# Eight level products and the values' transposes of an HGRN2 head moved later in TensorE's hand-written order of a head's second pair

## The chip, the cores and the metric

The kernel runs on one core of a Trainium2 chip. The metric is the device time of one execution in microseconds (us). TensorE multiplies (PE in the rows, PEld for its weight loads), VectorE is DVE, ScalarE is ACT, GpSimd is POOL, SyncE (SP) issues most DMAs.

## The reference

Two decoder layers over 512 prompt tokens and 8 x 4 sample tokens (544 columns), width 2048: an RWKV-7 layer and then an HGRN2 layer, each with a projection in, a recurrence, a gate and a projection out. The HGRN2 layer has 16 heads of 128 keys by 128 values. What matters here, cut down:

```python
q, f_logit, i, z = jnp.split(x @ w_in, 4, axis=-1)
f = lb + (1.0 - lb) * jax.nn.sigmoid(f_logit)
log_f = jnp.log(jnp.maximum(f, GATE_FLOOR))
k = (1.0 - lb) * jax.nn.sigmoid(-f_logit)
q = jax.nn.silu(q) * HGRN_DK ** -0.5
# per chunk and head, G = cumsum(log_f):
dec = jnp.where(mask, jnp.exp(jnp.minimum(G_t - G_s, 0.0)), 0.0)
A = jnp.einsum('bhtd,bhsd,bhtsd->bhts', q_c, k_c, dec)
o = A @ v_c + (q_c * exp(G)) @ S
S = exp(G_last) * S + (k_c * exp(G_last - G)).T @ v_c
...
o = o * lax.rsqrt(jnp.mean(o * o, axis=-1, keepdims=True) + NORM_EPS) * norm_w
out = (o * jax.nn.silu(z)) @ w_o
```

## The kernel before, in words

Everything stands channels by tokens: a tile of 128 output channels by 544 tokens, computed as two halves of 272 tokens in two banks. Matrix products are made of three passes with operands split in a high part (made by ScalarE, `_hi`) and a low part (made by VectorE as the difference, `_lo`): high x high, high x low, low x high.

HGRN2 needs four such tiles for each head: forget gate F, query qr, value v, gate zs. For heads e = 1 to 14 (14 heads) they are computed two at a time: pair 2e - 2 makes F and qr, pair 2e - 1 makes v and zs. `seven_products(q, steps)` is one pair. It computes a 2 x 2 block product (two output tiles, two halves of the tokens) over 12 of the 16 input tiles with seven products instead of eight, by sums of weight tiles and sums of token halves, and the other four input tiles (`rest`) in the plain way. Its order is written out by hand, in 58 sub-steps of three products of 128x272 each:

- product 0: sub-steps 1 to 6; product 1: 7 to 12; rest(0, 0): 13 to 16; rest(0, 1): 17 to 20
- product 2: 21 to 26; product 3: 27 to 32; product 4: 33 to 38; product 5: 39 to 44
- rest(1, 1): 45 to 48; product 6: 49 to 54; rest(1, 0): 55 to 58

The dictionary `steps` names a sub-step after which another piece of the head's work is put into TensorE's queue. TensorE works its queue in order, so a piece that has to wait holds up all that follows. The pieces are:

- `level(e, n)` for n = 0 to 7 (L1753, products at L1777, L1780, L1785, L1790): the products of keys and queries inside blocks that double from level to level. Level 0 needs the SiLU of qr; level 1 needs Q = qr x F; level n from 2 needs the keys and queries as `widen(e, n - 2)` left them (L2478, products at L2496, L2498, L2500 of VectorE), and the bank of level n - 2 taken over by `take(e, n - 2)` (L2502).
- `v_by_token`, `k_by_token` (L1794, L1806): transposes of values and keys; `kv` (L1815): products of the two. ScalarE copies the transposes out (`v_copy`, `k_copy`).
- `late(e - 1)` of the head before: two `outputs`, four `sample_out`, `sample_state`, and `norm`, which sums the squares of the head's output.

In the first pair of head e stand the keys' transposes and `kv` of head e - 1 and then its eight late pieces; in the second pair stand the eight levels of head e and the transposes of its values.

ScalarE and VectorE have their own orders written out, in `gates_pair(e, q)` and `values_pair(e, q)`. Both hold, between the head's own operations, what the products need: `item_hi`/`item_lo` (high and low part of one of seven weight items of 128x768, L1957 and L2300; item k is needed from product k on), `rest_hi`/`rest_lo` (128x512, L1965 and L2304), `weight_sum_1` to `_4` (VectorE), and the moves of finished sums out of the banks: `first_out` (L1969), `second_out` (L1973), `third_out` (L1977) on ScalarE, `upper_first` (L2338), `upper_fifth` (L2343), `upper_second` (L2348, L2351), `lower_second` (L2356, L2358), `lower_first` (L2362) on VectorE. Product 2 may start when `first_out` is done, as it adds onto the bank that this one copies:

```python
pe.wait_ge(s.p1, q + 1)
product(2, X, False)
```

On ScalarE, in `values_pair`, the order up to there is: item 2, SiLU of qr, `first_out`. In `gates_pair` the late part is `second_out`, item 5, `head_root` (Ln L2113 and Exp L2116 of what `norm` summed), item 6, rest, `third_out`, item 0 of the next pair, the two sigmoids, item 1 of the next pair; VectorE's `finish` stands after item 6 and ahead of `upper_second`. Before a function of another kind ScalarE loads a table (ACT_TABLE_LOAD in the rows).

SyncE loads a pair's two weight tiles (`next_weights`): the first once items 2 to 4 of the pair before are made, the second once item 6 is split. Heads 0 and 15 go through plain dense tiles, and the change doesn't touch them, but the last pair makes the high and low part of the dense tile behind it (`split_hi(GE)`, `split_lo(GE)`, 128x2048).

Of the kernel before, what the change touches and what calls it, by code (L numbers as in the profile page):

```python
# [1392 lines left out]
def trunk(nc, keep, d):  # L1393

    with ExitStack() as ctx:
# [10 lines left out]
        F, K, Q, qr, v, zs, sq, rs = (sb(n, [P, T]) for n in ("F", "K", "Q", "qr", "v", "zs", "sq", "rs"))  # L1406
# [47 lines left out]
        NQ = (GE - GS) // 2  # L1454
# [145 lines left out]
        def _(pe):  # L1600
# [48 lines left out]
            def seven_products(q, steps):  # L1649
                X, Y, V = (banks[(q + i) % 3] for i in range(3))  # L1650
                Z = banks[3]
                at = itertools.count(1)

                def three_passes(out, hi, lo, n, x, start):
                    w = slice(n * P, n * P + P)
                    for m, (a, b) in enumerate(((hi[:, w], x[0]), (hi[:, w], x[1]), (lo[:, w], x[0]))):
                        mm = pe.matmul(out, a, b, start=start and m == 0, stop=(m == 2), skip_group_check=True)  # L1657
                    return mm

                def then_step():  # L1660
                    m = next(at)
                    if m in steps:
                        steps[m]()

                def product(k, out, start):
                    pe.wait_ge(s.it_hi, ITEMS * q + k + 1)
                    pe.wait_ge(s.it_lo, ITEMS * q + k + 1)
                    hi, lo = item_slot(q, k)
                    for j in range(U):
                        mm = three_passes(out, hi, lo, j, operand(k, j), start and j == 0)  # L1670
                        if j == U - 1:
                            mm.then_inc(s.used, 1)
                        then_step()

                def rest(i, a, out, start, sem):
                    for n, kt in enumerate(range(2 * U, KT)):
                        mm = three_passes(out, c_hi[i], c_lo[i], n, base(kt, a), start and n == 0)
                        if sem and kt == KT - 1:
                            mm.then_inc(sem, 1)
                        then_step()  # L1680

                if q == 0:
                    pe.wait_ge(s.evac, GS - 1)
                    pe.wait_ge(s.t_lo, 2 * U)
                else:
                    pe.wait_ge(s.f0, q)
                product(0, X, True)
                if q:
                    pe.wait_ge(s.g1, q)
                product(1, Y, True)  # L1690
                pe.wait_ge(s.c_hi, 2 * q + 1)
                pe.wait_ge(s.c_lo, 2 * q + 1)
                rest(0, 0, Y, False, None)
                if q == 0:
                    pe.wait_ge(s.evac, GS)
                else:
                    pe.wait_ge(s.c12, q)
                rest(0, 1, Z, True, s.c_used)
                pe.wait_ge(s.p1, q + 1)
                product(2, X, False)  # L1700
                if q:
                    pe.wait_ge(s.evac, GS + 2 * q)
                product(3, V, True)
                pe.wait_ge(s.u2, q + 1)
                if q == 0:
                    pe.wait_ge(s.t3_lo, U)
                product(4, X, False)
                product(5, Z, False)
                pe.wait_ge(s.c_hi, 2 * q + 2)
                pe.wait_ge(s.c_lo, 2 * q + 2)  # L1710
                pe.wait_ge(s.up, q + 1)
                rest(1, 1, V, False, s.v_ready)
                pe.wait_ge(s.u3, q + 1)
                product(6, X, False)
                rest(1, 0, X, False, s.c_used)
# [78 lines left out]
            def v_by_token(e):  # L1794
                pe.wait_ge(s.evac, H0 + 4 * e + 3)
                if e:
                    pe.wait_ge(s.oln, 2 * e)
                else:
                    pe.wait_ge(s.rstd, 2)
                for c in range(4):  # L1800
                    pe.transpose(blk(tok_ps, c), blk(v, c), k.ident[:, :])  # L1801
                for h in range(2):
                    mm = pe.matmul(sm_ps[SMP * h:SMP * h + SMP, 0:P], v[:, SEQ:T], k.ident[:, :], start=True, stop=True)
                mm.then_inc(s.vt_mm, 1)
# [56 lines left out]
            def late(e):  # L1861
                return [lambda: outputs(e, 0), lambda: outputs(e, 2), lambda: sample_out(e, 0),
                        lambda: sample_out(e, 1), lambda: sample_out(e, 2), lambda: sample_out(e, 3),
                        lambda: sample_state(e), lambda: norm(e)]
# [8 lines left out]
            for e in range(KT):  # L1873
                n = H0 + 4 * e
                L = lambda m: (lambda: level(e, m))
                keys = [lambda: k_by_token(e - 1), lambda: kv(e - 1)]
                if 1 <= e < KT - 1:
                    steps = dict(zip((10, 13, 15, 17, 19, 21, 24, 27), late(e - 1)))
                    if e > 1:
                        steps.update(zip((2, 6), keys))  # L1880
                    seven_products(2 * e - 2, steps)
                    steps = {m: L(i) for i, m in enumerate((10, 12, 18, 24, 30, 36, 42, 48))}
                    seven_products(2 * e - 1, {**steps, 53: lambda: v_by_token(e)})
                    continue
                if e:
                    dense_evens_last(n, dict(zip((0, 2, 5, 6, 7, 8, 9, 10, 12, 15), keys + late(e - 1))))
                    dense(n + 1, {})
                at = (4, 5, 8, 11, 14) if e else (6, 7, 9, 12, 14)
                dense(n + 2, {kt: L(m) for m, kt in enumerate(at)})
                dense(n + 3, {1: L(5), 3: lambda: v_by_token(e), 6: L(6), 9: L(7), 12: lambda: k_by_token(e),  # L1890
                              15: lambda: kv(e)})
# [43 lines left out]
        def _(act):  # L1935
# [214 lines left out]
            def values_pair(e, q):  # L2150
                item_hi(q, 2)
                act.wait_ge(s.evac, H0 + 4 * e + 2)
                act.wait_ge(s.q1s, q)
                silu(qr, s.qr)
                act.wait_ge(s.vt_mm, e)
                first_out(q, v)
                item_hi(q, 3)
                item_hi(q, 4)
                rest_hi(q, 1)
                second_out(q, v)  # L2160
                item_hi(q, 5)
                item_hi(q, 6)
                if q < NQ - 1:
                    rest_hi(q + 1, 0)
                act.wait_ge(s.yz, e)
                third_out(q, zs)
                if q < NQ - 1:
                    item_hi(q + 1, 0)
                else:
                    split_hi(GE)  # L2170
                blocks_out(e)
                level_out(e, 6)
                if q < NQ - 1:
                    item_hi(q + 1, 1)
                level_out(e, 7)
                v_copy(e)

# [73 lines left out]
            for a in range(2):  # L2251
                for n in range(2):
                    m = KT - 2 + n
# [34 lines left out]
        def _(dve):  # L2288
# [283 lines left out]
            def values_pair(e, q):  # L2572
                lower_first(q - 1, qr)
                weight_sum_3(q)
                item_lo(q, 2)
                weight_sum_4(q)
                first_q(e)
                item_lo(q, 3)
                take(e, 0)
                widen(e, 0)  # L2580
                rest_lo(q, 1)
                item_lo(q, 4)
                take(e, 1)
                widen(e, 1)
                upper_first(q, v)
                take(e, 2)
                widen(e, 2)
                item_lo(q, 5)
                take(e, 3)
                widen(e, 3)  # L2590
                upper_fifth(q, v)
                item_lo(q, 6)
                take(e, 4)
                widen(e, 4)
                if q < NQ - 1:
                    rest_lo(q + 1, 0)
                    item_lo(q + 1, 0)
                else:
                    split_lo(GE)
                take(e, 5)  # L2600
                widen(e, 5)
                upper_second(q, v)
                if q < NQ - 1:
                    item_lo(q + 1, 1)
                widen(e, 6)
                lower_second(q, zs)
                if q < NQ - 1:
                    weight_sum_1(q + 1)
                    weight_sum_2(q + 1)
# [233 lines left out]
```

## Time and profile before

| | |
|---|---|
| Median of 3 runs | 2952.1 us (2946.95 to 2952.74) |
| Profiled execution | 2950.76 us, its span 2948.9 us |
| Mean granted TensorE clock | 0.969 of full speed |
| TensorE busy, products | 2759.2 us, 94% of the span |
| VectorE busy | 1592.5 us, 54% |
| ScalarE busy | 1260.1 us, 43% |
| GpSimd busy | 118.6 us, 4% |
| HBM | 91 GB/s over the span |

The profile is that of one execution. Busy time of TensorE is counted from the start of a product to its modelled end; products overlap, so a busy TensorE need not run at its full rate, and the clock must be read beside it. Times in the rows count from the span's start.

### The profile page before, as it was taken

The page shows a single profiled execution, that of the slowest core. Times are in us where ns is not written, and L with a number is a line of the kernel's source. Part 1 is how long each engine was busy: PE and PEld are TensorE (multiplying, and loading weights), DVE is VectorE, ACT ScalarE, POOL GpSimd, SP SyncE. Part 2 cuts the span into 40 slices and gives each one's busy share as a digit, 9 for nine tenths or more (in the row PEclk, how much of TensorE's full clock was granted, in tenths as well). Part 3 has the DMA queues.
Part 4 walks back from the last instruction along what each step waited for, and adds up shares of the span by engine and source line. Part 5 has one row for each costly group of instructions (what it writes and reads, how often), then busy time and mean ns, then how long its engine had stood idle before and what let it go on. Part 6 is the DMA issues. An engine that isn't in the chain of part 4 may idle for free. (4 is left out here: it accounts for less than half of the span.)

```text
span 2948.9 us, 82517 instructions
## 1 busy us (share of the span) xinstructions
PE 2759.2 (94%) x36816; PEld 2595.7 (88%) x36816; DVE 1592.5 (54%) x2703; ACT 1260.1 (43%) x1869; POOL 118.6 (4%) x92
## 2 busy tenths in 40 slices
PE   6999999999999999999799879989999998999997
PEld 5899999999997888887799778888888888888997
DVE  6334323333227788887522566666666666664324
ACT  5344424234225555555322454444444444444322
POOL 0000000000000000000000000000000000000000
PEclk8999999999999999999999989999999999999999
DMA  3333333333311111112222322322222222224323
GB/s 122 125 97 111 111 109 109 111 113 137 107 53 52 52 52 52 52 56 68 87 92 94 128 74 77 108 89 82 92 77 92 77 95 92 92 84 171 118 88 111
DMA packets 86816, 273.48 MB, mean 93 GB/s; under 512 B 16448, under 2 KB 29504, under 8 KB 65984
## 3 DMA queue, kind: packets, MB, share of 16 engines
q1 hardware_dynamic: 77248, 250.37, 25.5%
q10 hardware_dynamic: 9216, 17.83, 1.6%
q8 instruction: 292, 4.78, 0.7%
q14 instruction: 60, 0.49, 0.1%
HBM read 221.63 MB, written 46.54 MB: 91 GB/s over the span
## 5 line engine op out<-in xcount | busy, mean ns | idle before, releaser
L136 PE MATMUL w_pair<-a_x_hi,keep_w_hi 128*128 128x272 f32 x2016 | 427.4, 293 | 20.3 <-DVE a_x_lo L1059 19.4
L136 PE MATMUL w_pair<-a_x_lo,keep_w_hi 128*128 128x272 f32 x2016 | 418.7, 289 | 0.0
L136 PE MATMUL w_pair<-a_x_hi,keep_w_lo 128*128 128x272 f32 x2016 | 416.4, 288 | 0.0
L1045 DVE TENSOR_TENSOR keep_w_lo<-keep_raw,keep_w_hi 128x2048 fp32r<-128x2048 f32 x63 | 144.4, 2292 | 469.8 <-ACT keep_w_hi L798 469.8
L136 PEld LDWEIGHTS w_pair<-a_x_hi,keep_w_hi 128*128 128x128 f32 x2016 | 319.3, 189 | 26.7 <-issue 21.7
L136 PEld LDWEIGHTS w_pair<-a_x_lo,keep_w_hi 128*128 128x128 f32 x2016 | 317.1, 189 | 0.0
L136 PEld LDWEIGHTS w_pair<-a_x_hi,keep_w_lo 128*128 128x128 f32 x2016 | 316.9, 188 | 0.0
L136 PE MATMUL t_pair<-t_x_hi,keep_w_hi 128*128 128x272 f32 x1216 | 262.7, 298 | 27.1 <-DVE t_x_lo L2411 9.1
L136 PE MATMUL t_pair<-t_x_lo,keep_w_hi 128*128 128x272 f32 x1216 | 253.8, 290 | 0.0
L136 PE MATMUL t_pair<-t_x_hi,keep_w_lo 128*128 128x272 f32 x1216 | 253.6, 290 | 0.0
L136 PEld LDWEIGHTS t_pair<-t_x_hi,keep_w_hi 128*128 128x128 f32 x1216 | 193.0, 191 | 35.9 <-issue 19.9
L812 ACT ACTIVATE a_stage<-w_pair 128x544 f32<-128x544 f32 x64 | 40.0, 625 | 425.0 <-PE w_pair L136 425.0
L1657 PE MATMUL t_pair<-t_x_hi,u_it_hi 128*128 128x272 f32 x672 | 206.6, 307 | 0.0
L1657 PE MATMUL t_pair<-t_x_hi,u_it_lo 128*128 128x272 f32 x672 | 197.5, 294 | 0.0
L1657 PE MATMUL t_pair<-t_x_lo,u_it_hi 128*128 128x272 f32 x672 | 197.5, 294 | 0.0
L136 PEld LDWEIGHTS t_pair<-t_x_lo,keep_w_hi 128*128 128x128 f32 x1216 | 194.7, 191 | 0.0
L136 PEld LDWEIGHTS t_pair<-t_x_hi,keep_w_lo 128*128 128x128 f32 x1216 | 192.8, 190 | 0.0
L1657 PE MATMUL t_pair<-u_To,u_it_hi 128*128 128x272 f32 x896 | 183.6, 299 | 0.0
L1657 PEld LDWEIGHTS t_pair<-u_To,u_it_hi 128*128 128x128 f32 x896 | 140.7, 188 | 15.6 <-issue 13.4
L1657 PE MATMUL t_pair<-t_x_hi,u_c_hi 128*128 128x272 f32 x448 | 145.6, 325 | 0.0
L1657 PE MATMUL t_pair<-t_x_lo,u_c_hi 128*128 128x272 f32 x448 | 136.3, 304 | 0.0
L1657 PE MATMUL t_pair<-t_x_hi,u_c_lo 128*128 128x272 f32 x448 | 135.3, 302 | 0.0
(448 smaller groups left out, 6092.3 us busy)
## 6 DMA issues: line engine op xcount, KB each, us to landing
keep_raw<-in_w_in SPq DMA_DIRECT2D x64, 1024.0 KB, 5.0
keep_raw<-in_hgrn_in SPq DMA_DIRECT2D x64, 1024.0 KB, 5.1
keep_raw<-in_rwkv_wo SPq DMA_DIRECT2D x16, 1024.0 KB, 5.0
keep_raw<-in_hgrn_wo SPq DMA_DIRECT2D x16, 1024.0 KB, 5.0
t_Ss<-in_hgrn_s SPq DMA_DIRECT2D x16, 512.0 KB, 7.2
out_hgrn_s<-t_Sd SPq DMA_DIRECT2D x16, 512.0 KB, 7.7
scr_r<-a_stage ACTq DMA_DIRECT2D x16, 272.0 KB, 2.2
scr_k<-a_stage ACTq DMA_DIRECT2D x16, 272.0 KB, 2.1
```

The costliest lines, as they stand in the source:

```text
L136: mm = pe.matmul(out[:, a, 0:TH], w, x[:, kt, a * TH:(a + 1) * TH], start=(kt == order[0] and n == 0), stop=(kt == order[-1] and n == 2))
L812: act.activation(halves(stage[n % 2][:, :]), pair[3 if n == 2 else n % 2][:, :, 0:TH], func).then_inc(p.evac, 1)
L1045: dve.tensor_tensor(w_lo[b][:, :], raw[n % 2][:, :], w_hi[b][:, :].bitcast(F32), ALU.subtract).then_inc(p.raw_lo, 1)
L1657: mm = pe.matmul(out, a, b, start=start and m == 0, stop=(m == 2), skip_group_check=True)
```

## The change

In the second pair of a head the levels go from sub-steps 10, 12, 18, 24, 30, 36, 42, 48 to 22, 25, 31, 36, 41, 46, 51, 55, and the values' transposes from 53 to 58, the pair's last sub-step. In the first pair the keys' transposes and `kv` of the head before go from sub-steps 2 and 6 to 3 and 8, and its eight late pieces from 10, 13, 15, 17, 19, 21, 24, 27 to 13, 16, 18, 20, 22, 24, 27, 30. ScalarE makes the high part of the next pair's item 1 ahead of the copies of the finished blocks instead of between levels 6 and 7. VectorE's order in `values_pair` is written anew: `take` and `widen` of each level stand later among the low parts, and `lower_second` and item 1 of the next pair stand ahead of `take` 5. No operation is added or removed, and the order in which products are summed in a bank stays.

```diff
@@ TensorE @@
-                    steps = dict(zip((10, 13, 15, 17, 19, 21, 24, 27), late(e - 1)))
+                    steps = dict(zip((13, 16, 18, 20, 22, 24, 27, 30), late(e - 1)))
                     if e > 1:
-                        steps.update(zip((2, 6), keys))
+                        steps.update(zip((3, 8), keys))
                     seven_products(2 * e - 2, steps)
-                    steps = {m: L(i) for i, m in enumerate((10, 12, 18, 24, 30, 36, 42, 48))}
-                    seven_products(2 * e - 1, {**steps, 53: lambda: v_by_token(e)})
+                    steps = {m: L(i) for i, m in enumerate((22, 25, 31, 36, 41, 46, 51, 55))}
+                    seven_products(2 * e - 1, {**steps, 58: lambda: v_by_token(e)})
@@ ScalarE, values_pair @@
                 if q < NQ - 1:
                     item_hi(q + 1, 0)
+                    item_hi(q + 1, 1)
                 else:
                     split_hi(GE)
                 blocks_out(e)
                 level_out(e, 6)
-                if q < NQ - 1:
-                    item_hi(q + 1, 1)
                 level_out(e, 7)
@@ VectorE, values_pair @@
                 item_lo(q, 3)
+                rest_lo(q, 1)
+                item_lo(q, 4)
+                upper_first(q, v)
                 take(e, 0)
                 widen(e, 0)
-                rest_lo(q, 1)
-                item_lo(q, 4)
                 take(e, 1)
                 widen(e, 1)
-                upper_first(q, v)
+                item_lo(q, 5)
+                upper_fifth(q, v)
                 take(e, 2)
                 widen(e, 2)
-                item_lo(q, 5)
+                item_lo(q, 6)
                 take(e, 3)
                 widen(e, 3)
-                upper_fifth(q, v)
-                item_lo(q, 6)
-                take(e, 4)
-                widen(e, 4)
                 if q < NQ - 1:
                     rest_lo(q + 1, 0)
                     item_lo(q + 1, 0)
                 else:
                     split_lo(GE)
+                upper_second(q, v)
+                take(e, 4)
+                widen(e, 4)
+                lower_second(q, zs)
+                if q < NQ - 1:
+                    item_lo(q + 1, 1)
                 take(e, 5)
                 widen(e, 5)
-                upper_second(q, v)
-                if q < NQ - 1:
-                    item_lo(q + 1, 1)
                 widen(e, 6)
-                lower_second(q, zs)
```

## Rows read from the trace of the kernel before

**Rows 1.** The page, part 1: busy time, share, instructions of each engine.
```profile
PE 2759.2 (94%) x36816; PEld 2595.7 (88%) x36816; DVE 1592.5 (54%) x2703; ACT 1260.1 (43%) x1869; POOL 118.6 (4%) x92
```

**Rows 2.** TensorE's waits, 1750 to 2660: us in total, times, longest.
```profile
PE t_lev L1777 <- issue: 55.5, 14, 4.0
PE t_lev L1828 <- DVE t_S L2524: 2.5, 13, 0.2
PE t_lev L1790 <- DVE t_Q L2498: 1.2, 1, 1.2
```

**Rows 3.** The chain that ended last, whole span: start, us, what.
```profile
1773.39 15.49 PE t_pair L1657 x123
...
2615.97 15.49 PE t_pair L1657 x123
```

**Rows 4.** The same chain, from 2140 to 2210, one inner head.
```profile
2162.07 15.41 PE t_pair L1657 x123
2177.48 4.01 issue
2181.49 0.66 PE t_lev L1777 x26
...
2182.20 1.66 PE t_pair L1657 x6
...
2184.53 3.65 PE t_pair L1657 x18
...
2191.08 0.39 PE t_lev L1777 x32
2191.46 2.46 PE t_pair L1657 x18
...
2205.93 2.84 PE t_pair L1657 x21
```

**Rows 5.** Windows: stretch, length, busy time by engine, PEclk, DMA share, GB/s.
```profile
2177.50:2181.40 3.90, 0.00 (x0) 0.00 (x0) 3.71 (x6) 2.78 (x4) 0.00 (x0) 0.86 0.00 0
2181.50:2187.00 5.50, 5.50 (x85) 5.12 (x86) 4.51 (x10) 2.25 (x4) 0.00 (x0) 0.50 0.62 191
2187.20:2203.00 15.80, 15.80 (x253) 14.63 (x252) 10.67 (x30) 5.87 (x13) 1.90 (x1) 1.00 0.20 68
...
2654.90:2657.60 2.70, 1.50 (x12) 1.28 (x11) 2.70 (x6) 0.64 (x3) 0.00 (x0) 1.00 0.93 310
```

**Rows 6.** ScalarE's timeline, 2140 to 2210: start, us, line and operation.
```profile
2161.57 1.28 ACT L2113 ACT_TABLE_LOAD   x1
2162.86 0.87 ACT L2113 ACTIVATE t_rs<-t_tok,keep_eps 128x272 f32<-128x272 f32 x2
...
2180.73 0.66 ACT L2066 ACTIVATE t_qr<-t_qr 128x544 f32<-128x544 f32 x1
2181.29 0.37 ACT L1969 COPY t_v<-t_pair 128x272 f32<-128x272 f32 x1
...
2206.46 0.26 ACT L2091 COPY t_vtok<-t_tok 64x128 f32<-64x128 f32 x1
```

**Rows 7.** VectorE's timeline, 2140 to 2210, the same columns.
```profile
2198.06 0.68 DVE L2304 TENSOR_TENSOR u_c_lo<-keep_raw,u_c_hi 128x512 fp32r<-128x512 f32 x1
...
2199.37 0.96 DVE L2300 TENSOR_TENSOR u_it_lo<-keep_raw,u_it_hi 128x768 fp32r<-128x768 f32 x1 [0.62 <-ACT u_it_hi L1957]
2200.24 0.30 DVE L2509 COPY_PREDICATED t_Dg<-t_k_h_lev,t_lev 128x128 f32<-128x128 int32 x1
2200.44 0.42 DVE L2496 TENSOR_TENSOR t_K<-t_K,t_E 128x256 f32<-128x256 f32 x1
...
2201.19 0.43 DVE L2348 TENSOR_TENSOR t_v<-t_pair,t_v 128x272 f32<-128x272 f32 x1
2201.73 0.73 DVE L2351 TENSOR_TENSOR t_v<-t_v,t_rstd 128x544 f32<-128x544 f32 x1
```

**Rows 8.** DMA issues, 2170 to 2240: count, KB each, median us to landing.
```profile
keep_raw<-in_hgrn_in SPq DMA_DIRECT2D x4, 1024.0 KB, 5.3
```

## The prediction

> **What bounds the kernel now.** I read the page first: TensorE is busy for 2759.2 of 2948.9 us [rows 1], so only what stops or slows TensorE counts. Then the list of TensorE's waits over the stretch of the paired heads: one row carries it, 55.5 us in 14 waits of 4.0 us, all ahead of the first product of `level` (L1777) [rows 2]. The whole chain then gives the rhythm: the run that ends in this wait starts at 1773.39 for the first paired head and at 2615.97 for the fourteenth, so a head lasts (2615.97 - 1773.39) / 13 = 64.81 us [rows 3]. I take one inner head apart, around 2180 us, in the chain of that stretch [rows 4]. TensorE runs 41 sub-steps without a break (123 products in 15.41 us, 0.376 us a sub-step of three), stops at 2177.48 for 4.01 us, and then runs slowly: 6 products take 1.66 us and 18 take 3.65 us, where 18 take 2.46 us later on.
>
> The reason for the second loss is in the windows [rows 5]: the granted clock is 0.86 on average while TensorE stands still, 0.50 from 2181.5 to 2187.0 (the 1.2 GHz level) and 1.00 (2.4 GHz) after that. Against the full-rate rows (18 products and a restart 2.46, a middle level 0.39) the slow stretch costs 3.65 - 2.46 = 1.19 for the 18, 1.66 - 0.95 = 0.71 for the 6 (0.95 is 0.75 and a restart of 0.20), and by the same comparison about 0.5 for the two levels in it: 2.4 us. The stop itself costs 4.07 us: the 4.01 of the row, and the little by which two products otherwise overlap.
>
> What ends the stop: the timeline of ScalarE [rows 6]. Level 0 needs the SiLU of the queries, which starts at 2180.73 and ends at 2181.39; level 0 starts at 2181.49 [rows 4]. Followed back, the SiLU stands behind its table load, that behind the copy of item 2, which waits for VectorE's weight sum, and so on: sums, gate, sigmoids, `finish`, the head's Exp and Ln. That chain is a chain of ScalarE and VectorE and hangs on `norm` of the head before (sub-step 27 of the first pair), not on where level 0 stands.
>
> **The change, part by part.** I put all times in the clock of this head. The second pair starts (P1) 10 sub-steps ahead of 2177.48, at 2173.72.
>
> 1. Level 0 from sub-step 10 to 22. At full rate sub-step 20 ends at 2177.48 + 10 x 0.3765 = 2181.25. The stop at 10 is gone. Next late: product 2 begins at sub-step 21 and adds onto a bank that `first_out` has to copy out first, and `first_out` stands behind the SiLU on ScalarE: it started at 2181.29 and ended at 2181.66 [rows 6]. That is already after 2181.25.
>
> 2. `norm` from sub-step 27 to 30. From its end to P1 there are now 28 sub-steps instead of 31, so relative to P1 it ends at 2173.72 - 28 x 0.3765 = 2163.18 instead of 2162.07. Ln started at 2162.86, when its table load (2161.57, 1.28 us) was over and not when `norm` was [rows 4, 6]. Now `norm` is last: Ln at about 2163.25, and everything after it, down to the SiLU and `first_out`, comes 0.4 us later. I find no slack in that chain; where an engine waits, it waits for the other one. So `first_out` ends at 2182.06 and product 2 starts at 2182.16; it would have started at 2181.09, as a product starts about 0.16 us before the end of the one before it. New stop: 1.07 us. Bounds: 0.67 if the 0.4 us is absorbed; 2.35 if a whole table load (1.28) comes onto the chain. I take the chain as it adds up.
>
> The Trainium skill (ScalarE: Activation LUTs, What ACT_TABLE_LOAD costs) puts a switch at 2.66 us, 1.28 of load and 1.38 of drain. The rows show the function starting 1.29 us after its load [rows 6], so I take that; by the page (an estimate) the new stop would be 1.38 us longer in each head and the time 2896 us.
>
> 3. The levels at 25, 31, 36, 41, 46, 51, 55. TensorE needs 0.59 us more for a middle level (0.39 and a restart) [rows 4], and 0.64 for levels 0 to 2, which have a product for the sample tokens as well. Going on from product 2 at 2182.16: level 0 after sub-step 22 at 2183.05; sub-step 25 ends at 2184.82, 31 at 2187.72, 36 at 2190.24, 41 at 2192.71, 46 at 2195.18, 51 at 2197.65, 55 at 2199.75. VectorE has less room, as the levels now stand 5 sub-steps apart (2.47 us) and its other work lies between them. From level 4 on I add its queue in the new order, by start-to-start times of its rows (a row's duration less an overlap of 0.09) [rows 7]: `widen` 3 from 2193.17 (0.75), `rest_lo` 0.60 and `item_lo` 0.87 to 2195.39, `upper_second` 0.54 + 0.63 to 2196.56, `take` 4 0.20, `widen` 4 0.75 (its query product is done at 2197.52, in time for level 6), `lower_second` 0.83 (two half products like the first of `upper_second`), `item_lo` 0.87 to 2199.21, `take` 5 0.20, query product of `widen` 5 done at 2200.17. Level 7 needs that and starts at 2200.25 instead of 2199.70: a wait of 0.5 us. Earlier levels find their operands ready, by 0.8 us (level 2) or more. ScalarE's item copies and VectorE's low parts are ready for products 3 to 6 by a microsecond or more. Bounds of this term: 0 and, with another microsecond in VectorE's queue, 1.5 us.
>
> 4. `v_by_token` from 53 to 58, `k_by_token` from 2 to 3, `kv` from 6 to 8, outputs from 10 to 13. The products are the same, so TensorE's work stays. `v_copy` ends 0.8 us after the transposes (2206.72 against 2205.93) [rows 6]; three sub-steps and a restart give 1.33 us, so `k_by_token` finds it done, with 0.5 us to spare. The weight sums run 1 us later against the pair's start, but item 2 of the next pair is used 21 sub-steps on. S for the first outputs comes, by the same adding, about 5.9 us after the pair's start (before 5.7) and the outputs at sub-step 13 want it at 6.8 (before 5.5), so TensorE's small wait there goes (0.19 us idle, 2.5 us in 13 waits [rows 2]; with the restart 0.35 us of the pace).
>
> 5. DMA: nothing is added. The second weight tile of a pair may be loaded once item 6 has been split; that is now about 9 us ahead of the sum that reads it, and a load lands in about 5.3 us [rows 8]. SyncE's other waits (`sd`, `so_mm`, `yz`) move by at most 1.2 us.
>
> 6. The last paired head: `split_lo(GE)` (2048 columns) stood ahead of `take` 5 and held level 7 up for 1.2 us [rows 2]; now it stands ahead of `upper_second` and by the same adding holds level 6 up by about 0.8 us. With the hand-over to the next dense tile I give that head 1.3 us more gain than the others; the first head has no wait for S and gains 0.35 less.
>
> Sum for an inner head: removed 4.07 + 2.4 + 0.35 = 6.82, which would leave 64.81 - 6.82 = 58.0; added 1.07 + 0.5 = 1.57; net 5.25 us, a head of 59.6. Over 14 heads 73.5 us, plus 1.3 and less 0.35: 74.5 us. The profiled execution took 2950.8 us (span 2948.9 and 1.9 around it), 1.3 below the median 2952.1. So 2876.3 for such an execution, 2877.6 for the median; I forecast 2877.
>
> **The clock.** That the 2.4 us go rests on the stop of 1.07 us leaving the clock up. In this trace an idle of 1.25 us inside the window from 2654.90 kept a granted clock of 1.00 [rows 2, 5], while the 4 us stop lost it. The new stop is nearer to the former.
>
> **Rivals.**
> A: the clock still falls in each head, on the shorter stop together with the small level products behind it. It gives back 14 x 2.4 = 34 us: 2911. For it: the stop recurs every head and the levels follow at once. Against it: levels every 2.8 us run at 1.00 in the trace [rows 5]. The Trainium skill (TensorE: Matmul & The Clock Gate, What's actually happening and HAM oscillation) says the gate judges recent activity on a clock of its own, so by it some heads could fall and others not, between 2877 and 2911. Chance 0.12 for most heads falling.
> B: VectorE's queue is tighter than I add it: the levels wait 1 to 3 us in all per head, or the SiLU chain slips by a table load. 14 x 1.3 to 14 x 3 us back: 2895 to 2919. For it: I count 14 us of VectorE work in about 14.4 us. Chance 0.10.
> C, slower: the compressed stair. `take` and `widen` stand behind low parts that wait for ScalarE's copies, which wait for products 2 and 3, which now come after levels; if every level from 2 to 7 waits 1.3 us more (7.8 us a head), the head is 58.0 + 1.07 + 7.8 = 66.9 us and the time 2952 + 14 x 2 = 2981. It decides from 5.75 us of level waits a head; I add 0.5. Chance 0.03.
> D, no effect: the SiLU itself moves back with level 0, because it hangs on something that TensorE releases late in the pair. Then the 4 us only change their place: 2952. Against it: everything on ScalarE ahead of the SiLU is released before sub-step 10. Chance 0.02.
>
> **How the numbers follow.** Forecast 0.73, its own range 2856 (no stop at product 2 and no wait of level 7: 14 x 1.57 = 22 us less, 2855) to 2895. With A and most of B the range is 2856 to 2912. 0.2% of this kernel is 6 us, about what a measurement tells from no change. Faster 0.95 (forecast, A, B), same 0.02 (D), slower 0.03 (C).
>
> **What would show it.** The wait row of L1777 gone from 4.0 us; in its place an idle of about 1 us ahead of product 2, behind ScalarE's copy of `first_out` (L1969); a granted clock of 1.00 through the head; a head of 59 to 60 us; a wait of L1790 of a few tenths on VectorE's L2498; Ln starting at the end of `norm`. A granted clock near 0.95 over a head, or waits ahead of several levels, would make it wrong.

## The result and the profile after

The changed kernel takes 2883.64 us in the median of 4 runs (2882.63 to 2887.73), the kernel before 2952.42 us in 4 runs: a ratio of 0.9772, 95% interval 0.9755 to 0.9789, so 68.8 us or 2.3% faster. The forecast was 2877 with a range of 2856 to 2912. The profiled execution took 2883.76 us, its span 2882.0.

The page of the changed kernel, parts 1 and 2, against [rows 1]:

```profile
PE 2731.2 (95%) x36816; PEld 2568.2 (89%) x36816; DVE 1608.4 (56%) x2703; ACT 1259.1 (44%) x1869; POOL 117.8 (4%) x92
...
PEclk8999999999999999999999989999999999999998
```

TensorE's waits in the stretch of the paired heads, 1750 to 2600, changed kernel (in total, times, longest), against [rows 2]:

```profile
PE t_pair L1657 <- ACT t_v L1969: 11.2, 14, 0.9
PE t_lev L1790 <- DVE t_Q L2497: 6.4, 13, 0.5
PE t_lev L1785 <- DVE t_K L2495: 4.9, 12, 0.4
PE t_lev L1785 <- DVE t_Q L2497: 1.1, 1, 1.1
PE t_lev L1785 <- issue: 0.3, 1, 0.3
```

The row of 55.5 us is gone, and so is that of the paired heads' outputs (L1828). Three small waits stand in their place: product 2 for `first_out`, level 7 and level 6 for VectorE's widenings (VectorE's line numbers are one lower in the changed kernel). The rows of L1785 with 1.1 and 0.3 us are those of single heads; 1.1 is the last paired one.

The length of a head is best read from ScalarE's copy of the transposed values, which comes once in each. Timeline of ScalarE, changed kernel (start, us), heads 1, 6 and 7:

```profile
1815.91 0.59 ACT L2090 COPY t_vtok<-t_tok 128x512 f32<-128x512 f32 x1 [1.32 <-PE t_tok L1803]
...
2116.21 0.59 ACT L2090 COPY t_vtok<-t_tok 128x512 f32<-128x512 f32 x1 [1.33 <-PE t_tok L1803]
...
2176.25 0.59 ACT L2090 COPY t_vtok<-t_tok 128x512 f32<-128x512 f32 x1 [1.33 <-PE t_tok L1803]
```

The copy of head 13 starts at 2536.59: (2536.59 - 1815.91) / 12 = 60.06 us a head, where the same copy gives 64.83 in the kernel before. So an inner head gains 4.77 us. From the copy of head 0 to that of head 15 the gain is 68.0 us: 14 times 4.77, and 1.2 more. The part ahead of head 0's copy took 1.0 us longer in this execution (1748.8 us against 1747.8), which leaves the 66.9 by which the spans differ. All further heads are read in this way; a difference of 0.1 us a head shows there, while the copy of head 0 comes anywhere from 1743.6 to 1752.4 us in the traces here.

The granted clock, in windows of the changed kernel (columns as in [rows 5]):

```profile
2146.00:2153.00 7.00, 7.00 (x58) 7.00 (x58) 6.18 (x11) 1.98 (x3) 0.00 (x0) 1.00 0.49 173
2153.00:2154.80 1.80, 1.03 (x9) 0.81 (x7) 1.70 (x3) 1.79 (x4) 0.00 (x0) 1.00 0.00 0
2155.00:2156.00 1.00, 1.00 (x35) 0.85 (x38) 0.91 (x2) 1.00 (x2) 0.00 (x0) 1.00 0.36 57
```

The second window holds the stop ahead of product 2. The clock is at its upper level before, in and behind it, and 1.00 over the window from 1760 to 2560.

Where the levels wait: VectorE's timeline in the changed kernel,

```profile
2161.87 0.95 DVE L2299 TENSOR_TENSOR u_it_lo<-u_wS,u_it_hi 128x768 fp32r<-128x768 f32 x1
...
2163.45 1.41 DVE L2495 TENSOR_TENSOR t_K<-t_K,t_E 128x256 f32<-128x256 f32 x1
2164.78 0.41 DVE L2497 TENSOR_TENSOR t_Q<-t_Q,t_E 128x256 f32<-128x256 f32 x1
```

and GpSimd's at the same time:

```profile
2162.03 2.55 POOL L2277 TENSOR_TENSOR t_Sd<-t_Ss,t_E 128x1024 f32<-128x1024 f32 x1 [43.98 <-DVE t_E L2499]
```

The key product of `widen` 2, 0.42 us elsewhere [rows 7], takes 1.41 us. It starts while GpSimd's product for the sample states runs, and ends 0.28 us after that one does (2162.03 + 2.55 = 2164.58). In the kernel before, the same GpSimd product (2189.75, 1.90 us) fell mostly into time that VectorE spent waiting for a level.

### The profile page after: what moved, and what is told of

It is laid out like the page before. It is cut to its first block and busy times, and to the rows that moved or that the text cites. A ratio compares the mean times of both kernels' runs of the same rounds, so it can differ in the third digit from the quotient of the medians.

```text
span 2882.0 us, 82517 instructions
## 1 busy us (share of the span) xinstructions
PE 2731.2 (95%) x36816; PEld 2568.2 (89%) x36816; DVE 1608.4 (56%) x2703; ACT 1259.1 (44%) x1869; POOL 117.8 (4%) x92
## 5 line engine op out<-in xcount | busy, mean ns | idle before, releaser
L1045 DVE TENSOR_TENSOR keep_w_lo<-keep_raw,keep_w_hi 128x2048 fp32r<-128x2048 f32 x63 | 144.4, 2293 | 470.1 <-ACT keep_w_hi L798 470.1
L1657 PE MATMUL t_pair<-t_x_hi,u_it_hi 128*128 128x272 f32 x672 | 200.5, 298 | 0.0
L1657 PE MATMUL t_pair<-t_x_hi,u_c_hi 128*128 128x272 f32 x448 | 135.6, 303 | 0.0
L798 ACT CAST keep_w_hi<-keep_raw 128x2048 fp32r<-128x2048 f32 x63 | 120.2, 1908 | 31.0 <-ACT a_stage L812 28.0
L2293 DVE TENSOR_TENSOR keep_w_lo<-keep_raw,keep_w_hi 128x2048 fp32r<-128x2048 f32 x38 | 87.1, 2292 | 82.2 <-ACT keep_w_hi L1945 82.2
```

What stands on the lines that cost most here:

```text
L798: act.copy(w_hi[2 if n == 2 else n % 2][:, :], raw[n % 2][:, :]).then_inc(p.raw_hi, 1)
L1045: dve.tensor_tensor(w_lo[b][:, :], raw[n % 2][:, :], w_hi[b][:, :].bitcast(F32), ALU.subtract).then_inc(p.raw_lo, 1)
L2293: dve.tensor_tensor(w_lo[g % 2][:, :], raw[g % 2][:, :], w_hi[g % 2][:, :].bitcast(F32), ALU.subtract).then_inc(s.raw_lo, 1)
```

## The experiments

**Is the long row GpSimd's doing?** `sd_later`:

```diff
+ pool.wait_ge(s.o_mm, e + 1)        # heads 1 to 14, and behind Vm
  pool.tensor_tensor(Sd[:, :, :], Ss[:, :, :], E[2]...)
```

GpSimd makes its product for the sample states later here: behind its product `Vm` of the sample tokens' values, and once the head's outputs are done.

> The changed kernel with one edit: for heads 1 to 14 GpSimd's product for the sample states (t_Sd, 128x1024) waits for the head's outputs in the next pair instead of starting behind the second widening. Theory 1: the key product of the third widening takes 1.41 us instead of 0.42 because GpSimd's product runs at the same time, and this 1.0 us in VectorE's queue makes the wait of level 6 (0.41 us). Then that row falls back to 0.42, level 6 no longer waits, level 7 still waits about 0.5 us, a head takes 59.5 instead of 60.04 us and the time is 7 us less, about 2877. Rival: the long row has another cause, or the queue has other room; then a head stays at 60.0 and the time at 2884.

2874.97 us, ratio 0.9747 (0.9733 to 0.9762); a head of 59.65 us. TensorE's waits, 1750 to 2660:

```profile
PE t_pair L1657 <- ACT t_v L1969: 11.8, 14, 0.9
PE t_lev L1790 <- DVE t_Q L2507: 6.4, 13, 0.5
PE t_lev L1828 <- DVE t_S L2533: 1.1, 1, 1.1
PE t_lev L1785 <- DVE t_Q L2507: 0.8, 1, 0.8
```

and the key products of `widen` 2 and `widen` 3 in VectorE's timeline:

```profile
2156.70 0.42 DVE L2505 TENSOR_TENSOR t_K<-t_K,t_E 128x256 f32<-128x256 f32 x1
...
2159.18 0.43 DVE L2505 TENSOR_TENSOR t_K<-t_K,t_E 128x256 f32<-128x256 f32 x1 [0.50 <-PE t_lev L1777]
```

The product is back at 0.42 us and level 6 waits in the last paired head alone. Level 7 waits as before. GpSimd's product cost 0.41 us of a head, the wait of level 6, as theory 1 has it. Most of the other 0.6 us of its 1.0 lay in slack: without it `widen` 3 waits 0.50 us for level 4, and with it `widen` 3 doesn't wait.

**Does the wait of product 2 cost what it shows?** `first_out_first`, and `both_moves` with both edits:

```diff
                 item_hi(q, 2)
+                act.wait_ge(s.vt_mm, e)
+                first_out(q, v)
                 act.wait_ge(s.evac, H0 + 4 * e + 2)
                 act.wait_ge(s.q1s, q)
                 silu(qr, s.qr)
-                act.wait_ge(s.vt_mm, e)
-                first_out(q, v)
```

> The changed kernel with one edit: in the second pair ScalarE copies the first sum out (first_out) ahead of the queries' SiLU instead of behind it. Theory 1 (the waits add up): the wait of product 2, 0.8 us a head, goes, and up to 0.3 us comes back at level 0; 14 x 0.6 = 8 us less, about 2875. Theory 2 (VectorE's queue sets the end of the pair): TensorE comes earlier to levels 6 and 7 and waits there for what it gained at product 2; the time stays within 3 us of 2884, and the waits of L1785 and L1790 grow from 0.4 and 0.5 us to 1.7 us together.

> The changed kernel with both edits: GpSimd's sample-state product behind the next pair's outputs, and first_out ahead of the SiLU. If the two costs are separate they add: a head of 58.9 us, about 2868. If VectorE's queue sets the end of the pair, it is the better of the two alone and no more: 2875 to 2877.

`first_out_first`: 2873.65 us, ratio 0.9742 (0.9726 to 0.9758), a head of 59.41. `both_moves`: 2871.03 us, ratio 0.9733 (0.9719 to 0.9748), a head of 59.00. TensorE's waits of `both_moves`:

```profile
PE t_lev L1790 <- DVE t_Q L2507: 6.5, 13, 0.5
PE t_lev L1777 <- issue: 3.3, 14, 0.2
```

0.65 us for the one edit, 0.41 for the other, 1.06 for the two: they add. (The whole times, 10.0, 8.7 and 12.6 us under the changed kernel's, scatter too much to show it.) The waits of levels 6 and 7 did not take up the gain (6.8 and 6.4 us in all with `first_out_first`, 6.3 and 6.4 in the changed kernel). Theory 2 falls, and for a reason that I should have seen: in the changed kernel `widen` 1 waits 0.63 us for level 2 (VectorE, 2160.95), so VectorE's queue comes earlier when TensorE does. With `first_out_first` that wait is gone and the 0.65 us are gained; the slack was just enough.

**Whose order brings the gain?** `tensor_order_only` is the kernel before with the four lines of TensorE from the diff and nothing else.

> The kernel before with TensorE's new sub-steps alone (levels, transposes, late pieces), ScalarE and VectorE in their old order. Theory 1: the whole gain is TensorE's order; in the old order of VectorE 2.9 us of its other work stand behind the fifth widening, so levels 6 and 7 find their operands ready (0.9 us a head less than in the changed kernel), and the weight sums come 1.3 us later, which costs 0.4 us at the next head's first outputs: a head of about 59.5 us, 2876. Rival: the new order of ScalarE and VectorE is what makes the later levels possible; without it their waits grow by a microsecond or more a head and the time is over 2892.

2926.07 us, ratio 0.9911 (0.9891 to 0.9931); a head of 62.95 us. My theory 1 is wrong by 3.4 us a head, and the rival is right in kind, though not as to the place: of the 4.77 us only 1.88 come without the other engines' orders. TensorE's waits, 1750 to 2660:

```profile
PE t_tok L1818 <- ACT t_ktok L2096: 21.9, 13, 1.7
PE t_pair L1657 <- DVE u_it_lo L2300: 19.2, 14, 1.4
PE t_pair L1657 <- ACT t_v L1969: 11.6, 14, 0.9
```

Levels 6 and 7 don't wait, as I expected, but two other pieces do. Product 5 waits for item 5's low part, which in the old order stands behind `widen` 2, and that waits for level 3, now 12 sub-steps later. And `kv` waits for the copy of the keys: `lower_second`, item 1 and the weight sums stand behind `widen` 5 and 6, so item 2, the SiLU of the gate and `k_copy`, all behind them on ScalarE, come late. Two rows of VectorE's timeline show a share of GpSimd in both waits:

```profile
2184.34 0.76 DVE L2496 TENSOR_TENSOR t_K<-t_K,t_E 128x256 f32<-128x256 f32 x1 [0.86 <-PE t_lev L1777]
...
2198.96 1.80 DVE L2312 TENSOR_TENSOR t_wS<-keep_raw 128x768 f32<-128x768 f32 x1
```

The key product of `widen` 2 is 0.34 us longer than alone, beside GpSimd's product for the sample states, and `weight_sum_1` takes 1.80 us instead of 0.95 beside its product `Vm` (2198.90 to 2199.94). Both stand ahead of what TensorE waits for, so by this trace up to 0.34 of the 1.4 us and up to 0.85 of the 1.7 us are GpSimd's. No run here moves `Vm` to show it.

`item5_first` is that kernel with one line of VectorE moved:

```diff
                 upper_first(q, v)
+                item_lo(q, 5)
                 take(e, 2)
                 widen(e, 2)
-                item_lo(q, 5)
                 take(e, 3)
```

> TensorE's new sub-steps with the old orders of the other engines (tensor_order_only, 62.95 us a head), and one move on VectorE: item 5's low part ahead of take 2 and widen 2. Theory 1: product 5 waited 1.4 us only because that low part stood behind a widening that waits for level 3, itself moved 12 sub-steps later; with it ahead the wait goes and a head takes 61.4 us, while the wait of kv (1.7 us) for the keys' copy stays. Rival: VectorE is simply short of time in the second pair, so the wait turns up at another low part or level; 62.5 to 63 us.

2912.3 us in one run, a head of 62.15 us: 0.80 us less instead of 1.55. Product 5 still waits, 0.56 us. VectorE's timeline says why:

```profile
2172.72 2.52 DVE L2300 TENSOR_TENSOR u_it_lo<-u_wS,u_it_hi 128x768 fp32r<-128x768 f32 x1
```

This low part, 0.94 us in `tensor_order_only`, took 2.52 us; in its new place it falls onto GpSimd's product (2172.53 to 2174.43). So the queue was the cause of more than half of the first wait (0.81 of 1.37 us). That GpSimd is the cause of the rest is read from this row: the low part is 1.57 us late, more than the 0.56 us that are left. It wasn't tested by a run. `kv` waits as before (21.9 us).

**From which stop on is the clock lost?** Three kernels differ from the changed one in the sub-step of level 0 alone, 18, 16 and 13 for 22:

```diff
-enumerate((22, 25, 31, 36, 41, 46, 51, 55))
+enumerate((16, 25, 31, 36, 41, 46, 51, 55))
```

> The changed kernel with level 0 after sub-step 18: a stop of about 1.3 us, and 0.6 us more a head than the changed kernel. With the stop of 2.1 us the clock was lost in 3 of the heads, with 3.2 us in most, with 0.8 us in none. Theory 1: whether a stop loses the clock depends on its length and on where it falls; 1.3 us loses it in none or one of 14 heads: 60.6 us, about 2892. Rival: it is lost as often as with 2.1 us; three heads are longer by 1.4 us or more.

> The changed kernel with one number altered: level 0 after sub-step 16 of the second pair instead of 22. TensorE then stops there for about 2.1 us until the SiLU is done, and the stop at product 2 (0.8 us) goes; product 2 and all behind it come 1.3 us later. Theory 1: a stop of 2.1 us leaves the clock at 1.00; a head takes 61.3 us, about 2902 in all. Rival: a stop of 2 us is enough to lose the clock, and the 2.4 us of slow products come back in each head: 63.7 us, about 2935.

> The changed kernel with level 0 after sub-step 13: a stop of about 3.2 us. In the kernel before the clock was lost about 2.8 us into the stop (mean 0.86 over 3.9 us). Theory 1: so it is lost here too; 2.4 us later at product 2 and 2.4 us of slow products: a head of 64.8 us, about 2951. Rival: the clock holds through 3.2 us; 62.4 us, about 2917.

One run each: 2886.2, 2901.1 and 2939.7 us, with stops of 1.4, 2.1 and 3.3 us in each of the 14 heads. With 1.4 us every inner head takes 60.36 us and the clock is 1.00. With 2.1 us three of the 14 stops lose the clock and eleven keep it; the inner heads take 61.12 us at a clock of 1.00 and 62.6 at 0.97. With 3.3 us there are three kinds. Over the 6 us behind the stop the granted clock is 1.00 in two heads, 0.72 in three and 0.50 to 0.52 in nine, the last nine in a row; the inner heads take 62.24, 63.75 and 64.7 to 64.9 us. Windows of `level0_at_16`, first one head that kept the clock and one that lost it, then the stop and what follows in each:

```profile
1937.28:1998.40 61.12, 58.02 (x635) 54.16 (x636) 43.67 (x83) 29.01 (x50) 3.58 (x2) 1.00 0.28 93
1998.40:2060.95 62.55, 59.45 (x635) 55.59 (x636) 43.74 (x83) 29.01 (x49) 3.58 (x2) 0.97 0.28 91
...
1912.50:1914.50 2.00, 0.00 (x0) 0.00 (x0) 1.90 (x3) 1.99 (x3) 0.00 (x0) 1.00 0.00 0
1914.60:1917.60 3.00, 3.00 (x55) 2.96 (x56) 2.60 (x5) 2.11 (x4) 0.00 (x0) 1.00 0.58 158
...
2034.80:2036.70 1.90, 0.00 (x0) 0.00 (x0) 1.79 (x3) 1.89 (x3) 0.00 (x0) 1.00 0.00 0
2036.80:2039.80 3.00, 3.00 (x44) 2.94 (x45) 2.61 (x5) 2.14 (x4) 0.00 (x0) 0.50 0.57 156
```

The two stops are alike, and so is the work around them; behind one the clock is at its upper level, behind the other at the lower one for some 3 us. So length alone does not decide. For 2.1 us the rival was right in 3 heads of 14 and theory 1 in 11; for 3.3 us, where I had said lost in every head, five of 14 kept it wholly or in part. The Trainium skill (TensorE: Matmul & The Clock Gate, What's actually happening) says that the gate looks at recent activity in step with a clock of its own, which does not start with the kernel: by that rule equal stops may end differently, and the trace agrees.

**The rest of the chain.** `norm_at_27` is the changed kernel with the late pieces earlier:

```diff
-dict(zip((13, 16, 18, 20, 22, 24, 27, 30), late(e - 1)))
+dict(zip((12, 14, 16, 18, 19, 21, 24, 27), late(e - 1)))
```

> The changed kernel with the late pieces at sub-steps 12, 14, 16, 18, 19, 21, 24, 27 instead of 13 to 30. Theory 1: norm is done before Ln's table load again, so Ln, the SiLU and first_out come 0.4 us earlier against the second pair's start; the wait of product 2 falls from 0.80 to 0.4 us, a head from 60.04 to 59.6, about 2878. Rival 1: the outputs, one sub-step earlier, wait for S again and give it back. Rival 2: the 0.4 us is taken up by VectorE's queue and shows as longer waits of levels 6 and 7: 60.0.

2880.63 us, ratio 0.9764 (0.9746 to 0.9782), a head of 59.70. ScalarE's timeline of the changed kernel, the table load ahead of Ln, and Ln:

```profile
2133.02 1.28 ACT L2113 ACT_TABLE_LOAD   x1
2135.95 0.86 ACT L2113 ACTIVATE t_rs<-t_tok,keep_eps 128x272 f32<-128x272 f32 x2 [1.64 <-PE t_tok L1858]
```

The same two of `norm_at_27`:

```profile
2128.12 1.28 ACT L2113 ACT_TABLE_LOAD   x1
2129.41 0.87 ACT L2113 ACTIVATE t_rs<-t_tok,keep_eps 128x272 f32<-128x272 f32 x2
```

Ln waits 1.64 us for `norm` in the one and for nothing but its table in the other, where ScalarE's own queue ahead of it comes last. The wait of product 2 falls from 11.2 to 6.5 us in all, and those of the levels stay. 0.36 us a head, for which I had said 0.4; the gain in the whole time, 3 us, is within what the runs scatter.

`level7_ready` is `both_moves` with VectorE's `take(e, 5)` and `widen(e, 5)` ahead of `lower_second` and item 1; `all_four` is that with the late pieces of `norm_at_27`:

```diff
+take(e, 5)
+widen(e, 5)
 lower_second(q, zs)
 if q < NQ - 1:
     item_lo(q + 1, 1)
-take(e, 5)
-widen(e, 5)
 widen(e, 6)
```

> Both earlier edits (GpSimd's sample-state product behind the next outputs, first_out ahead of the SiLU) and, on VectorE, take 5 and widen 5 ahead of lower_second and of item 1's low part. Theory 1: level 7 finds its operand; its wait of 0.5 us with the lost overlap goes and a head falls from 59.0 to 58.4 us, about 2862 to 2865. Rival: lower_second and item 1 now come too late for product 1 of the next pair, and the wait only moves there: 59.0.

> The four moves together: level7_ready, and the late pieces at sub-steps 12 to 27. Theory 1: the SiLU comes 0.4 us earlier against the pair, so the last wait, 0.2 us of level 0, goes with its lost overlap: a head of 58.2 us instead of 58.47, 3 to 4 us less in the stretch of the heads (too little for the time of a whole run). Rival: it gives nothing, as in the stretch some other chain holds 58.47.

2861.53 us (0.9697, 0.9675 to 0.9720) with a head of 58.48, and 2855.22 us (0.9677, 0.9661 to 0.9693) with a head of 58.13. TensorE's waits of `all_four`, 1750 to 2660:

```profile
PE t_lev L1828 <- DVE t_S L2533: 1.1, 1, 1.1
PE t_lev L1785 <- DVE t_Q L2507: 0.8, 1, 0.8
```

Both stand in the last paired head and behind it. The inner heads run without a wait that the list shows. `all_four` is 96.2 us or 3.2% faster than the kernel before the change, measured beside it at 2951.43 us, and faster than the changed kernel too.

## Why the prediction was right, and where it was off

The mechanism was right and the size off by 6.6 us, most of it in one term. That the stop and the lost clock were what the change removed is shown by putting them back. The changed kernel with level 0 at sub-step 13, and nothing else altered, stops for 3.3 us in each head and loses the clock in most; a head then takes 64.8 us, and 62.24 where it keeps the clock, against 60.06 in the changed kernel and 64.83 in the kernel before.

- **The stop at level 0** (4.07 us) is gone in all 14 heads, and product 2 waits for `first_out` behind the SiLU, as forecast. I had 0.91 us of idle; it is 0.80 (11.2 / 14).
- **The slow products** (2.4 us) are gone, with the clock at 1.00. Stops of 0.8 us (the changed kernel) and 1.4 us (`level0_at_18`) kept it in all 14 heads, so rival A did not come about. But my argument for it, the length of one other idle, was thin: of equal stops of 2.1 us three in 14 lost the clock.
- **`norm` later**: the 0.4 us are there (0.36 by `norm_at_27`), by way of Ln as said. The stop longer by 1.38 us (2896 us) is not: SiLU starts 1.29 us after the start of its table load here too (2152.53 and 2153.82).
- **Level 7** waits 0.50 us, as said.
- **Level 6** waits 0.41 us, and I had it ready, by 0.13 us (2197.52 against 2197.65). This is the term that failed. I summed VectorE's queue from `widen` 3 on, as if that began when level 4 was done, and took `widen` 2 ahead of it as it ran in the kernel before, 0.42 us a product; GpSimd was left out. The steps of the queue are right in number and order; one product ahead of the sum is 1.0 us longer. It was rival B's mechanism, a tighter queue on VectorE, below the size that I gave it.
- **The sum**: undone one after the other, product 2 costs 1.00 us a head (0.65 by `first_out_first`, 0.35 by the earlier late pieces of `all_four`), level 7 0.52 (`level7_ready`) and level 6 0.41 (`sd_later`), over 58.13 us in `all_four`: 60.06. I had 1.07, 0.5, nothing, and 58.0: 59.6. Level 6 makes 14 x 0.41 = 5.7 of the 6.6 us.
- **Transposes, keys and outputs** moved without a wait, and the small wait of the outputs went, as said.
- **The last paired head** gained 66.11 - 60.21 = 5.9 us between value copies, 1.1 more than an inner one (forecast 1.3). Level 6 waits 1.1 us there behind `split_lo(GE)` (forecast 0.8); with GpSimd's product out of the way, in `sd_later`, it waits 0.8.
- **The first paired head** was to gain 0.35 us less; no such loss shows in the 68.0 us from the copy of head 0 to that of head 15.
- **Rival C** did not come about, but `tensor_order_only` shows its mechanism at work: low parts behind widenings that wait for levels. What keeps it away in the changed kernel is the new order of VectorE and ScalarE (no run parts the two), whose value I had put at nothing in that run's expectation, 3.4 us a head too low. With TensorE's new order and the old ones of the others I had added up the levels, and not what stands behind them.
- **Rival D** did not come about: the SiLU did not move back with level 0.

The reverse, the new orders of ScalarE and VectorE with TensorE's old sub-steps, can't run: `take` 0 and `widen` 0 would stand behind `upper_first`, which waits for sub-step 20, while level 2 at sub-step 18 waits for `widen` 0. So 1.88 and 2.89 us are the shares in this one order of steps, not values of either part by itself.

## What to carry to other kernels

When a piece that waits is moved later in one engine's queue, add up every other engine's queue again from that piece on, and look for operations that now stand behind it; here the reordering of the other engines, on top of the move, was worth 2.9 us a head, and the move alone 1.9. Take the durations for that sum from a stretch with the same neighbours: a product of VectorE with both inputs in SBUF took 0.42 or 1.41 us according to what GpSimd ran beside it. And a stop of TensorE of 2.1 us cost its own length or 1.45 us more, from one repetition to the next of the same program.

## What the runs showed of the hardware

- A VectorE product with both inputs in SBUF doesn't run beside GpSimd's: 1.41 us for 0.42, ending 0.28 us behind GpSimd's, and in `item5_first` 2.52 us for 0.95, ending 0.81 us behind GpSimd's (2172.72 + 2.52 against 2172.53 + 1.90). Both are as if it had begun 0.14 us before GpSimd's end. GpSimd's product, 1.90 us alone, took 2.55 when one of VectorE's had started first. In the changed kernel `weight_sum_3` (2177.15) takes 1.77 us for 0.95 in the same way, beside GpSimd's `Vm` (2177.07 to 2178.10); TensorE has no wait from it there. The VectorE operations that ran meanwhile with an input in PSUM kept their times. The Trainium skill (SBUF — State Buffer, SBUF: two separate sides) states it: the two share a port pair that one of them holds for a whole instruction. The trace agrees; I had not applied it in the prediction.
- Equal stops of TensorE of 2.1 us kept the clock in eleven heads of 14 and lost it in three. Of those of 3.3 us, nine lost it for the whole slow stretch, three for a part, and two kept it; of those of 0.8 and 1.4 us none in 14 lost it; of those of 4.0 us in the kernel before all 14 did.
